# A 26,000-instruction block stack on one core: eight places where the order of the work changes

## The reference

```
x = first_block(x, ...)      # attention and gated linear attention, then 32 experts, top 4
x = second_block(x, ...)     # the case's "second" stage
x = third_block(x, ...)      # "even", "ffn0", "odd", "ffn1", final norm

# second_block: gated delta rule in chunks of 64, beside a causal attention
decay = exp(where(causal, g[i] - g[j], -inf))
a     = where(strict, (k_beta @ k.T) * decay, 0)
t_inv = inverse(eye + a)                       # unit lower triangular, 64 x 64
mixed = (gate_dn * y_dn + gate_mb * y_mb) @ w_out
x     = x + gate * rms_norm_2(mixed, g_post)

# odd mixer (mLSTM): 8 heads, one output product over 1024 features
hc = mlstm_scan(q, k, v, ig, lf)               # needs the scans of the gates
o  = head_rmsnorm(hc, norm_g) * sigmoid(og)
y  = o @ w_out
# feed-forward, twice
a, g = split(h @ w_in);  a = causal_dwconv(a)
y    = (gelu(a) * g) @ w_out                   # 2816 features in
# modulations of a layer
mod = silu(c) @ ada_w + ada_b
```

## Time and profile before

| | |
|---|---|
| median of three runs | 2452.07 us |
| the profiled execution | 2452.29 us |
| its span (first to last instruction) | 2450.5 us |
| PE busy | 2239.5 us, 91% |
| VectorE busy | 856.4 us, 35% |
| ScalarE busy | 414.8 us, 17% |
| mean granted clock of TensorE | 0.965 of full |

### The profile page before, as it was taken

One profiled execution on the slowest core, in us unless ns is written; L12 is line 12 of the kernel. 1 busy time (PEld: TensorE's weight loads), 2 busy tenths in 40 slices (PEclk: granted clock), 3 DMA queues, 4 the chain that ended last, 5 costly groups with the idle time before them and its releaser, 6 DMA issues. The chain is left out here.

```text
span 2450.5 us, 25702 instructions
## 1 busy us (share of the span) xinstructions
PE 2239.5 (91%) x10084; PEld 1304.7 (53%) x10084; DVE 856.4 (35%) x1744; ACT 414.8 (17%) x895; POOL 108.8 (4%) x79
## 2 busy tenths in 40 slices
PE   7998999988999888888879999998799999989998
PEld 4655443333334333333337788665568866448873
DVE  4564222122213221212127457444548202345201
ACT  1223111111111111111121322122321001222100
POOL 1000000000000000000000000000100000000000
PEclk8998999999999999999989999999899999999999
DMA  9767498999999999999977752446227543426441
GB/s 351 271 243 311 175 368 315 412 412 413 412 348 412 412 412 413 412 412 412 413 284 280 261 210 104 171 160 218 69 90 272 188 155 126 150 71 230 155 163 43
DMA packets 212511, 657.22 MB, mean 268 GB/s; under 512 B 8590, under 2 KB 13302, under 8 KB 195668
## 3 DMA queue, kind: packets, MB, share of 16 engines
q1 hardware_dynamic: 208528, 649.53, 69.5%
q0 software_dynamic: 1808, 3.65, 0.4%
q10 hardware_dynamic: 2004, 1.67, 0.2%
HBM read 653.77 MB, written 1.05 MB: 267 GB/s over the span
## 5 line engine op out<-in xcount | busy, mean ns | idle before, releaser
L1658 PE MATMUL ps<-w,XE 128*64 128x512 f32 x1280 | 347.2, 606 | 47.0 <-DMA w<-in_w_gate_up 29.2
L817 PE MATMUL ps<-HF,w 128*128 128x256 f32 x1280 | 280.7, 382 | 0.0
L817 PEld LDWEIGHTS ps<-HF,w 128*128 128x128 f32 x1280 | 245.0, 192 | 35.3 <-issue 1.9
L1688 DVE TENSOR_TENSOR T<-ps,BB 128x512 f32<-128x512 f32 x64 | 44.3, 692 | 590.8 <-PE ps L1658 590.8
L1658 PEld LDWEIGHTS ps<-w,XE 128*64 128x64 f32 x1280 | 112.2, 139 | 259.0 <-issue 251.4
L1729 PE MATMUL ps<-w,AT 128*64 128x512 f32 x640 | 179.2, 613 | 25.6 <-DMA w<-in_w_down 13.5
L817 PE MATMUL ps<-HT,w 128*128 128x256 f32 x704 | 164.9, 393 | 4.4 <-DVE dqk L2450 3.7
L639 DVE SCALAR_TENSOR_TENSOR AUX<-w,CS,AUX 128x512 f32<-128x512 f32 x210 | 157.9, 752 | 7.5
L856 PE MATMUL ps<-w,AF 128*128 128x512 f32 x352 | 151.8, 593 | 1.8 <-DVE AF L3142 1.8
L817 PEld LDWEIGHTS ps<-HT,w 128*128 128x128 f32 x704 | 136.8, 197 | 25.9 <-issue 6.2
L856 PE MATMUL ps<-w,HT 128*128 128x512 f32 (+1 forms) x352 | 149.1, 579 | 0.3 <-DVE S L1502 0.3
(11 more groups left out here) (604 smaller groups left out, 2703.6 us busy)
## 6 DMA issues: line engine op xcount, KB each, us to landing
w<-in_w_gate_up SPq DMA_DIRECT2D x80, 2048.0 KB, 22.3
w<-in_w_down SPq DMA_DIRECT2D x40, 2048.0 KB, 22.4
w<-in_ada_w SPq DMA_DIRECT2D x24, 2048.0 KB, 8.9
w<-in_ffn_w_in SPq DMA_DIRECT2D x20, 2048.0 KB, 8.0
w<-in_w_in SPq DMA_DIRECT2D x17, 2048.0 KB, 9.4
tables<-in_w_gate_up SPq DMA_DIRECT2D x16, 2048.0 KB, 24.0
GR<-in_w_gate_up SPq DMA_DIRECT2D x16, 2048.0 KB, 23.7
AUX<-in_w_gate_up SPq DMA_DIRECT2D x16, 2048.0 KB, 23.7
```

Source lines behind the costliest of these rows:

```text
L817: ins = e.matmul(out_, w[:, k, c:c + n], HT[:, k, :], start=k == 0, stop=k == kc - 1, skip_group_check=True)
L1658: ins = e.matmul(b[j * n:j * n + n, :], FM.XE[:, side(x), 4 * kh + k, j * n:j * n + n], ring.tile(512, 1024, "gu", ex_, h, kh, x[0])[:, k, ...
L1688: e.tensor_tensor(FM.T1[:, :], bank(x, "gu", q), FM.BB[:, q * 512:q * 512 + 512], ADD).then_inc(*dve())
```

## The change

Eight edits. (1) In `second_pe` the sums 16 and 17 stand behind the groups cv1 and cv2 instead of before them. (2) In `inverse_dve` the products of mask, beta, k k^T and the second mask are taken at step 1 without the exponential, into W6 and Y, and step 2 multiplies by the exponential twice (once for `U`, once for `aT`): eight VectorE instructions instead of seven. (3) The output of second is made by `out_part_pe`: the first group starts on features 0 to 3, after a wait for the first half of MX. (4) `ada_sum_pe(29)` stands before `norm_turn_pe` instead of behind it. (5) In layer 0 of the feed-forward the sums 38 and 39 stand behind fg0 and fg1, and VectorE stores them between the products of the fg groups. (6) Each of the three parts of a feed-forward output waits for its own groups' products. (7) In odd the transposes of the gates stand behind ov0, VectorE copies them behind the convolution of group 1, and ScalarE's exponential of them stands behind the copy of ov0. (8) The output of odd is made by halves of features: transposes of the first heads before the last quarter of og, three groups over features 0 to 3, transposes of the second heads, the rest; the transposes of the normalised x stand before the last feature tile of the last group.

```diff
@@ -385,6 +385,7 @@
     bank = Banks(ps, at)
+    begun = {}
     ring = Ring(m.SLOTS, slots, at, 4)
@@ -879,7 +880,22 @@
-    def out_pe(e, tag, parts, OT, hook=None):
+    def out_part_pe(e, tag, OT, hf, t, ks=range(8)):
+
+        w = ring.tile(1024, 512, tag, hf, 0)
+        new, done = (tag, hf, t) not in begun, begun.get((tag, hf, t), 0) + len(ks) == 8
+        begun[(tag, hf, t)] = begun.get((tag, hf, t), 0) + len(ks)
+        b = bank.take(e, tag, hf, t, hold=True) if new else bank(tag, hf, t)
+        if t == 0 and new:
+            e.wait_ge(*at("w", tag, hf, 0))
+        ins = tok_pe(e, b, w[:, ks[0]:ks[-1] + 1, :], 0, 512, OT, t, ks[0], new, done)
+        if done:
+            ins.then_inc(*pe(tag, hf, t))
+            bank.drop(tag, hf, t)
+            if t:
+                pe.leave("w", tag, hf, 0)
+
+    def out_pe(e, tag, parts, OT, hook=None, ready=None):
@@ -893,6 +909,8 @@
                 e.wait_ge(*at("w", tag, hf, s))
+            if ready is not None and (hf, t) == (0, 0):
+                ready(e, s)
             if hook is not None and (hf, t, s) == order[-1]:
@@ -2429,20 +2447,21 @@
             e.tensor_scalar(W5[t], W5[t], 0.0, None, MIN).then_inc(*dve("d diff", t))
-        if s == 2:
-            e.wait_ge(*at("d exp", t))
-            e.tensor_tensor(heads(W6[t], 4), heads(W5[t], 4), bc(C("SU64"), 4), MUL).then_inc(*dve())
-            own(e, dve)
-            e.tensor_tensor(W6[t], W6[t], bank("db", t), MUL).then_inc(*dve())
+            e.tensor_tensor(heads(W6[t], 4), heads(bank("db", t), 4), bc(C("SU64"), 4), MUL).then_inc(*dve())
             dve.leave("bank", "db", t)
...
             e.wait_ge(*at("dkq", t))
-            e.tensor_tensor(p.aT[:, :], bank("dk", t), W6[t], MUL).then_inc(*dve())
+            e.tensor_tensor(W6[t], bank("dk", t), W6[t], MUL).then_inc(*dve())
             dve.leave("bank", "dk", t)
             own(e, dve)
-            e.tensor_tensor(heads(W6[t], 4), heads(p.aT[:, :], 4), bc(C("H1"), 4), MUL).then_inc(*dve())
+            e.tensor_tensor(heads(p.Y[:, :], 4), heads(W6[t], 4), bc(C("H1"), 4), MUL).then_inc(*dve())
+        if s == 2:
+            e.wait_ge(*at("d exp", t))
             own(e, dve)
-            e.tensor_tensor(heads(p.U[:, :], 4), bc(ident, 4), heads(W6[t], 4), SUB).then_inc(*dve("U", t, 0))
+            e.tensor_tensor(p.Y[:, :], p.Y[:, :], W5[t], MUL).then_inc(*dve())
+            own(e, dve)
+            e.tensor_tensor(heads(p.U[:, :], 4), bc(ident, 4), heads(p.Y[:, :], 4), SUB).then_inc(*dve("U", t, 0))
+            e.tensor_tensor(p.aT[:, :], W6[t], W5[t], MUL).then_inc(*dve())
         if s == 3:
@@ -2540,8 +2559,8 @@
         for g in (1, 2):
+            feats_pe(e, ("cv", g), (f"cv{g}",), ring.tile(1024, 512, f"cv{g}"), 4, F2.HT)
             ada_sum_pe(e, 15 + g)
-            feats_pe(e, ("cv", g), (f"cv{g}",), ring.tile(1024, 512, f"cv{g}"), 4, F2.HT)
         ada_sum_pe(e, 18)
@@ -2600,10 +2619,15 @@
             feats_pe(e, ("proj", i), ("proj", i), ring.tile(512, 512, "proj", i), 4, F2.OT[:, 0:4, :])
-        e.wait_ge(*at("mx"))
-        out_pe(e, "out2", ((1024, 0),), F2.MX)
+        e.wait_ge(*at("mx", 0))
+        out_part_pe(e, "out2", F2.MX, 0, 0, range(4))
+        e.wait_ge(*at("mx", 1))
+        out_part_pe(e, "out2", F2.MX, 0, 0, range(4, 8))
+        out_part_pe(e, "out2", F2.MX, 1, 0)
+        out_part_pe(e, "out2", F2.MX, 0, 1)
+        out_part_pe(e, "out2", F2.MX, 1, 1)
+        ada_sum_pe(e, 29)
         norm_turn_pe(e, m.even, "even", 0)
-        ada_sum_pe(e, 29)
         enter_pe(e, m.even, "even", "eqa", ("eqa",))
@@ -2812,7 +2836,7 @@
             own(e, dve)
-            e.tensor_tensor(mx, mx, SG[hf][:, 1, :, :], ADD).then_inc(*dve("mx"))
+            e.tensor_tensor(mx, mx, SG[hf][:, 1, :, :], ADD).then_inc(*dve("mx", hf))
         post_norm_dve(e, "out2", 2, m.even, "even", 3, parts=((0, 0), (1, 0)), early=True)
@@ -3085,16 +3109,20 @@
                 continue
-            if i <= len(FFN_ADA[layer]):
+            if i < 5 and i <= len(FFN_ADA[layer]):
                 ada_sum_pe(e, FFN_ADA[layer][i - 1])
...
             feats_pe(e, key, key, ring.tile(1024, 128 * n, *key), n, f.HT)
-        e.wait_ge(*at("fglu", layer))
+            if layer == 0 and name == "fg" and g < 2:
+                ada_sum_pe(e, 38 + g)
+
+        def ready(e, s):
+            e.wait_ge(*at("fglu", layer, 2 * s + 1))
         if layer == 0:
-            out_pe(e, ("outf", 0), FFN_PARTS, f.A, lambda e: norm_turn_pe(e, m.odd, "odd", 0))
+            out_pe(e, ("outf", 0), FFN_PARTS, f.A, lambda e: norm_turn_pe(e, m.odd, "odd", 0), ready)
             enter_pe(e, m.odd, "odd", ("oqk", 0), ("oqk", 0))
         else:
-            out_pe(e, ("outf", 1), FFN_PARTS, f.A)
+            out_pe(e, ("outf", 1), FFN_PARTS, f.A, None, ready)
         end(pe, "pe", tag)
@@ -3117,6 +3145,8 @@
                 ada_acc_dve(e, FFN_ADA[layer][0])
+            elif layer == 0 and g == 5:
+                ada_acc_dve(e, 39)
             elif g < len(FFN_ADA[layer]):
@@ -3131,15 +3161,15 @@
                                            op1=ADD).then_inc(*dve("fconv", layer, g))
-        if layer == 0:
-            ada_put_dve(e, 39)
         for g, n in GROUPS:
+            if layer == 0 and g in (2, 3):
+                ada_put_dve(e, 36 + g)
             e.wait_ge(*at("gelu", layer, g if g else 5))
...
                 o = f.A[:, 4 * g + j, :]
-                e.tensor_tensor(o, o, half(j, ("fg", layer, g)), MUL).then_inc(*dve("fglu", layer))
+                e.tensor_tensor(o, o, half(j, ("fg", layer, g)), MUL).then_inc(*dve("fglu", layer, g))
                 if j % 2:
@@ -3216,14 +3246,14 @@
         feats_pe(e, ("oqk", 1), ("oqk", 1), ring.tile(1024, 512, "oqk", 1), 4, FO.HT, odd_gates_pe, 2)
+        toks_pe(e, ("ov", 0), ("ov", 0), ring.tile(1024, 512, "ov", 0), FO.HT)
         b = bank.take(e, "ccm")
...
         ins.then_inc(*pe("ccm"))
-        for hf in range(2):
-            toks_pe(e, ("ov", hf), ("ov", hf), ring.tile(1024, 512, "ov", hf), FO.HT)
+        toks_pe(e, ("ov", 1), ("ov", 1), ring.tile(1024, 512, "ov", 1), FO.HT)
         for g in range(2):
@@ -3255,13 +3285,35 @@
                     ins.then_inc(*pe("mo", g, t, i))
+        odd_heads_pe(e, 0)
         og_piece_pe(e, 3, range(4, 8))
-        for g in range(2):
-            odd_heads_pe(e, g)
-        features(e, "OTo")
-        out_pe(e, "outo", ((1024, 0),), FO.HT, lambda e: norm_turn_pe(e, m.ffn[1], "ffn1", 0))
+        e.wait_ge(*at("OTo", 0, "act"))
+        e.wait_ge(*at("OTo", 0, "dve"))
+        for hf, t in ((0, 0), (1, 0), (0, 1)):
+            out_part_pe(e, "outo", FO.HT, hf, t, range(4))
+        odd_heads_pe(e, 1)
+        out_part_pe(e, "outo", FO.HT, 1, 1, range(4))
+        e.wait_ge(*at("OTo", 1, "act"))
+        e.wait_ge(*at("OTo", 1, "dve"))
+        for hf, t in ((0, 0), (1, 0), (0, 1)):
+            out_part_pe(e, "outo", FO.HT, hf, t, range(4, 8))
+        out_part_pe(e, "outo", FO.HT, 1, 1, range(4, 7))
+        norm_turn_pe(e, m.ffn[1], "ffn1", 0)
+        out_part_pe(e, "outo", FO.HT, 1, 1, range(7, 8))
         enter_pe(e, m.ffn[1], "ffn1", ("fa", 1, 0), ("fa", 1, 0))
         end(pe, "pe", "odd")
+
+    def heads_turned_act(e, g):
+        e.wait_ge(*at("OTo", 4 * g))
+        for j in range(4 * g, 4 * g + 2):
+            e.activation(FO.HT[:, j, :], half(j, "OTo"), ACT.Copy, scale=V("odd_norm_g_3", j)).then_inc(*act("OTo", g, "act"))
+        act.leave("bank", "OTo", 4 * g)
+
+    def heads_turned_dve(e, g):
+        e.wait_ge(*at("OTo", 4 * g + 2))
+        for j in range(4 * g + 2, 4 * g + 4):
+            e.tensor_scalar(FO.HT[:, j, :], half(j, "OTo"), V("odd_norm_g_3", j), None, MUL).then_inc(*dve("OTo", g, "dve"))
+        dve.leave("bank", "OTo", 4 * g + 2)
@@ -3274,14 +3326,14 @@
             copy_feats_act(e, ("oqk", g), 4, lambda j, p: e.activation(FO.CI[:, j, 3:259], p, ACT.Copy))
-            if g:
-                e.wait_ge(*at("ccm", "in"))
-                e.activation(FO.CCM[:, :, 8:16], FO.CCM[:, :, 8:16], ACT.Exp).then_inc(*act("ccm", "exp"))
             e.wait_ge(*at("oconv", g))
...
             copy_toks_act(e, ("ov", hf), lambda t, p: e.activation(FO.VX[:, t, 4 * hf:4 * hf + 4, 0:128], heads(p, 4), ACT.Copy))
+            if hf == 0:
+                e.wait_ge(*at("ccm", "in"))
+                e.activation(FO.CCM[:, :, 8:16], FO.CCM[:, :, 8:16], ACT.Exp).then_inc(*act("ccm", "exp"))
         wf = FO.W[:, :, :].rearrange("p i t -> p (i t)")
@@ -3294,17 +3346,14 @@
                     e.activation(FO.dn[:, 0:2], bv[:, :, 128], ACT.Abs).then_inc(*act("mo abs", g, t, i))
+            if g:
+                heads_turned_act(e, 0)
             og_piece_act(e, 2 * g + 1)
...
                              st[:, 44 + 8 * g + 4 * t:48 + 8 * g + 4 * t])
-        for k in (0, 4):
-            e.wait_ge(*at("OTo", k))
-            for j in range(k, k + 2):
```

(16 more changed lines are left out.)

## The result

The changed kernel took 2421.16 us (median of 4 runs, 2418.07 to 2422.28), the kernel before, run beside it, 2449.9 us (2446.49 to 2452.66). The ratio is 0.9883 with a 95% interval of 0.9871 to 0.9894: 28.7 us less. The forecast was 2424.0, with 2417 to 2432 as its range. The profiled executions differ by a little more: 2420.92 against 2452.29 us, their spans 2419.1 against 2450.5. PE is busy for 2232.1 us, 92% of the span, at a mean granted clock of 0.968 against 0.965.

A forecast was written before the change was run, and what follows sets the result against it. PE, busy 91% of the span, was taken as the bound, so only its waits and the 1.2 GHz stretches behind them could be won. The eight edits' terms summed to 28.3 us, from 2452.29 to 2424.0 us, range 2417 to 2432.

The forecast's parts named there:

- the forecast 1.4: Before sum 18, ahead of zd: PE waits 1.4 us for VectorE, limiting edit 1 to 2.6 us.
- the account of tile 0: Inverse: tile 0's gain is lost in VectorE's wait for tile 1's exponential, so step 3 begins only 0.2 us earlier.
- Rival C: Inverse: if PE waited for `U`, 1.4 us and the clock behind, 1.6, would be gained: 2421; chance 7%.
- The sum ahead of the transposes: Entry of the even stage: with sum 29 ahead of the transposes, PE enters 0.5 us later than before.
- The term rested on the load: Feed-forward, edit 5: fg0's load lands about 1899.7, PE waits 1.1 us for it; gain 7.5 us.
- the forecast wait of 0.9 at the end: After odd's output, before ffn1: PE ends at 2201.8 and enters the next stage at 2202.7.
- A: Rival: waits left or new cost clock as the old ones did, 2.0 us at each of four sites: 2432; chance 10%.
- the four sites named: Waits left or new: 1.4 us before sum 18, 1.8 before even, 1.1 before fg0, 0.9 before ffn1.
- the ground of the forecast against A: Waits of 2.11 and 1.31 us cost no clock; waits of 2.30 us and more did.
- The third of such sites: By the skill's freely running clock window, a third of the short-wait sites could lose clock: 2427.
- B: Rival: loads become the bound, fg0 or cv2 landing later; 5 us and the clock's 3: 2432; chance 6%.
- D: Rival: the denser PE is throttled behind 1904, slower than before, 2457 at 0.06 less clock; chance 3%.

The follow-up runs named there:

- the early product: Changed kernel with two VectorE products of the inverse (mask times exponential, times q k^T) moved from step 3 to the end of step 2: 2415.82 us.
- the small moves: Changed kernel with sum 18 behind zd, sum 38 ahead of fa5, even's norm turn ahead of sum 29, last output turned behind feature 5: 2417.75 us.

## Why the prediction was right, and where it was not

| edit | forecast | measured | by |
|---|---|---|---|
| 1 | 2.6 | 2.7; 0.8 | before/changed; undone, both with a loss in the entry |
| 2 | 0.2 | 0.1 | stretch b less the 16 records, undone |
| 3, 4 | 1.6 | 2.0 | stretch c, at equal clock, twice |
| 5 | 7.5 | 7.1; 7.6 | stretch e, with the clock lost by before; undone |
| 6 | 1.8 | 2.3 | 1.2 in each layer, before/changed |
| 7 | 6.1 | 6.5; 5.8 | stretch f, before/changed; undone |
| 8 | 8.5 | 8.9; 9.2 | stretch h, before/changed; undone |
| sum | 28.3 | 27.0 to 30.4 | |

The medians say 28.7. The profiled executions differ by 31.4: by before/changed the edits make 29.7, and 1.8 is clock in places that no edit touches, where before lost 1.6 more in a, 1.3 in d and 0.2 in the entry, and changed 1.3 more in g and 0.1 in b. The prediction took the profiled execution of before for a typical one. It was 2.4 us above the median of the four runs, and that is most of the 2.8 us by which 2424.0 was too high. That the sum of the terms came within 0.4 us of the medians is in part luck: by the two profiles the same edits brought 1.4 more than forecast.

**Edit 1.** The wait of 1.39 before sum 18 is the forecast 1.4. The term is right for the execution that was read, and too high for one in which PE loses clock in the entry: the wait that is removed is then 0.73, not 2.30. The prediction took the wait for a property of the order. It is the time until VectorE's last addition, and that addition waited 2.43 us for the load of `g_post`, which the prediction did not look at.

**Edit 2.** Who waits was right, and decided it: PE waited for the bank of q k^T. So was the account of tile 0, whose gain is lost in the wait for `deR`. The term is 0.11 instead of 0.2; of the difference 0.07 stands between L2457 and L2461, which start 0.79 us apart in the changed kernel (1473.55 and 1474.34) where two products that wait for each other are 0.72 to 0.73 apart. Rival C, PE waiting for `U`, is excluded by the 1.90 us that are still there and by the early product, which removes them.

**Edits 3 and 4.** The sum ahead of the transposes costs 0.3 to 0.4, not 0.5, and the output's 2.11 went whole. The rest of the 2.0 is in how the records lie: one that follows another without a wait starts 0.16 us before the end of the one in front (2147.39 against 2146.51 + 1.04), so that a wait of 2.11 taken away brings 2.27, and the output's 64 records take 27.63 instead of 27.73. 2.27 + 0.10 - 0.34 = 2.03, between edits 3 and 4 undone and edit 7 undone, which both kept their clock there. The wait at the entry is 1.64 and no longer names `st` but `HE` on ScalarE, as worked out.

**Edit 5.** The term rested on the load: fg0 cannot start before it lands. PE waits 1.09 for it, and the clock stays at 1.00. Since the load was the limit, the sum taken away from before fa5 brought nothing, which the small moves then showed.

**Edit 6.** The waits of 0.91 went, and each brought more than its length, by the same 0.16 and 0.10: from the second XF transposes of the last layer to the start of its output it is 150.94 us before and 149.87 in the changed kernel (149.86 or 149.87 in all eleven profiles with the edit), and the output's 176 records take 75.80 and 75.70, so 1.2 us. In the first layer before and edit 5 undone show only 0.7 (236.0 and 235.3), since the second lost 0.5 us more clock behind its wait of 4.9. Edit 6 was not undone by itself; both figures are from kernels that differ in other places too.

**Edits 7 and 8.** Mechanisms as forecast. In edit 8 the forecast wait of 0.9 at the end is 0.79, and no wait stands at the two turns; the 0.4 to 0.7 us that the edit brought beyond the forecast are not accounted for.

**The rivals.** A, new short waits that cost clock, did not come true in the changed kernel's profile: the windows behind the four sites named are at 1.00. It came true once elsewhere. The wait before the even stage (1.64 or 1.65 us) stands in eight profiles; in seven the 48 records behind it took 5.60 us, and with edit 5 undone, whose program is the same up to there, 7.22:

```profile
1612.11 7.22 PE L845 MATMUL ps<-HE,w 128*128 128x128 f32 x48 [1.65 <-ACT HE L981]
```

So the ground of the forecast against A, that single waits below 2.30 us lose no clock, does not hold, as the last section also shows; that none was lost at these sites in the measured profile is in part luck. The third of such sites for which A gave 2427 has no source in the rows. B did not happen: PE's only wait for a load in the changed places is the 1.09, and cv2's load landed in time. D, a denser PE throttled, did not happen either: 140.00 of 140.00 us busy are at 1.00, twice.

## What to carry to other kernels

Read the releaser of a wait before pricing what is in front of it: edit 2 shortened a chain of which PE waited only for the end, and two products moved into an idle hole of VectorE gave 6 us. Price a small edit by the stretch between two events with the same work, in several profiles, and not by the span, which here gave the wrong sign once. When a wait between two engines goes, take the clock that falls behind it into the price, and read what the releaser itself waited for: the 2.30 us of PE before sum 16 were a load's, through VectorE, and shrank to 0.73 when that load landed 1.6 us sooner behind its issue.
